# Pairs of experts as fp32 column strips between the units of a dense expert

## The reference

```python
def hierarchical_moe(h, w_rg, b_rg, w_re, b_re, w1, w3, w2):
    t = h.reshape(b * s, d)
    p_group = jax.nn.softmax((t @ w_rg + b_rg).astype(jnp.float32), axis=-1)
    g_val, g_idx = lax.top_k(p_group, 1)
    fine = (t @ w_re + b_re).astype(jnp.float32).reshape(-1, N_EXPERT_GROUPS, EXPERTS_PER_GROUP)
    ...
    for e in range(N_EXPERTS):
        y_e = (jax.nn.silu(t @ w1[e]) * (t @ w3[e])) @ w2[e]
        out = out + combine[:, e:e + 1] * y_e
    return out.reshape(b, s, d)
```

## Time and profile before

| | us |
| --- | --- |
| timed runs | 1611.56, 1608.8, 1608.3 |
| median | 1608.8 |
| span of the profiled execution | 1604.0 |
| PE busy in the span | 1547.5 (96%) |
| DVE, ACT busy | 1090.1 (68%), 838.2 (52%) |
| last matmul of the program, end | 1600.4 |

### The profile page before, as it was taken

How to read it: one execution, slowest core, us unless ns; L and a number is a source line. 1 busy time by engine, 2 the same in 40 slices (tenths; PEclk the granted TensorE clock), 3 DMA queues, 4 the chain that set the end, 5 groups by cost and what they waited for, 6 DMA issues and landing times.

```text
span 1604.0 us, 24065 instructions
## 1 busy us (share of the span) xinstructions
PE 1547.5 (96%) x8757; PEld 1261.9 (79%) x8757; DVE 1090.1 (68%) x1726; ACT 838.2 (52%) x1342; POOL 14.0 (1%) x36
## 2 busy tenths in 40 slices
PE   6999999999999999999999999998998999999999
PEld 3865558988888889888659999886776888889888
DVE  3447764854444446878977676887775687786894
ACT  4326554722322325688864544654453566666672
POOL 2000000000000000000010000000000000000000
PEclk9999999999999999999999999999999999999999
DMA  9588633422332332434525665543220789788792
GB/s 350 162 346 312 247 122 103 153 71 92 103 93 93 103 99 59 122 90 131 173 64 171 192 187 186 171 152 96 93 92 1 263 298 380 247 329 311 256 380 81
DMA packets 195799, 279.69 MB, mean 174 GB/s; under 512 B 12434, under 2 KB 111220, under 8 KB 190588
## 3 DMA queue, kind: packets, MB, share of 16 engines
q1 hardware_dynamic: 194308, 274.21, 50.6%
q0 software_dynamic: 1152, 4.19, 0.7%
q10 hardware_dynamic: 248, 0.09, 0.0%
HBM read 277.40 MB, written 1.05 MB: 174 GB/s over the span
## 4 chain that ended last, share of the span: by engine, by line
PE 76%; DVE 10%; ACT 7%; DMA 3%; issue 2%; SPq 0%; POOL 0%; DVEq 0%; ACTq 0%; POOLq 0%
PE bank L443 66%; DVE weights_lo L408 2%; PE bank L1540 2%; DMA ada_rows_in<-in_ada_w_dram 2%; PE bank L745 1%; ACT weights_hi L396 1%; PE bank L1381 1%; PE bank L1365 1%; DVE work L2781 1%; DVE softmax_cols L2648 1%; PE bank L1349 1%; ACT work L2118 1%; DVE x_and_ctx L590 1%; DMA stage<-in_lru_w_i_dram 1%; DVE work L2639 1%
## 5 line engine op out<-in xcount | busy, mean ns | idle before, releaser
L408 DVE TENSOR_TENSOR weights_lo<-stage,weights_hi 128x1024 fp32r<-128x1024 f32 x324 | 385.1, 1220 | 48.4 <-ACT weights_hi L396 44.6
L396 ACT ACTIVATE weights_hi<-stage 128x1024 fp32r<-128x1024 f32 x324 | 330.1, 1056 | 114.3 <-PE bank L443 69.4
L443 PE MATMUL bank<-act_hi,weights_hi 128*128 128x256 f32 (+1 forms) x1040 | 324.6, 312 | 1.3 <-DVE act_lo L553 1.0
L443 PE MATMUL bank<-act_lo,weights_hi 128*128 128x256 f32 (+1 forms) x1040 | 323.1, 311 | 0.0
L443 PE MATMUL bank<-act_hi,weights_lo 128*128 128x256 f32 (+1 forms) x1040 | 323.1, 311 | 0.0
L443 PE MATMUL bank<-weights_hi,ff_hi 128*128 128x512 f32 x568 | 221.6, 390 | 0.2 <-DVE ff_lo L3031 0.2
L443 PE MATMUL bank<-weights_hi,ff_lo 128*128 128x512 f32 x568 | 221.1, 389 | 0.0
L443 PE MATMUL bank<-weights_lo,ff_hi 128*128 128x512 f32 x568 | 221.0, 389 | 0.0
L443 PEld LDWEIGHTS bank<-act_hi,weights_hi 128*128 128x128 f32 x1040 | 198.3, 191 | 14.5 <-DVE act_lo L553 1.5
L443 PEld LDWEIGHTS bank<-act_lo,weights_hi 128*128 128x128 f32 x1040 | 198.3, 191 | 11.2
L443 PEld LDWEIGHTS bank<-act_hi,weights_lo 128*128 128x128 f32 x1040 | 198.3, 191 | 10.5
(11 more groups left out here) (404 smaller groups left out, 2018.5 us busy)
## 6 DMA issues: line engine op xcount, KB each, us to landing
stage<-in_mlp_w_dram SPq DMA_DIRECT2D x128, 512.0 KB, 4.0
stage<-in_w_dram SPq DMA_DIRECT2D x96, 512.0 KB, 6.1
ada_rows_in<-in_ada_w_dram SPq DMA_DIRECT2D x40, 1024.0 KB, 6.5
x_and_ctx<-in_w_dram SPq DMA_DIRECT2D x48, 512.0 KB, 5.9
work<-in_w_dram SPq DMA_DIRECT2D x48, 512.0 KB, 6.2
stage<-in_w_in_dram SPq DMA_DIRECT2D x32, 512.0 KB, 4.2
stage<-in_lru_w_in_dram SPq DMA_DIRECT2D x20, 512.0 KB, 3.9
stage<-in_attn_w_qkv_dram SPq DMA_DIRECT2D x12, 512.0 KB, 7.9
```

The lines of the kernel that those rows point to most:

```text
L396: act.eng.activation(whi[u % NRING][:], landing(act, u)[:], ACT.Copy).then_inc(sem("hi_ready"), 1)
L408: dve.eng.tensor_tensor(wlo[u % NRING][:], landing(dve, u)[:], whi[u % NRING][:].bitcast(F32), ALU.subtract).then_inc(sem("lo_ready"), 1)
L443: m = pe.eng.matmul(ps, l, r, start=start and j == 0, stop=stop and j == 2, skip_group_check=True)
```

## The change

The groups are ranked by their number of tokens. The largest (rank 0) is dense, ranks 1 and 2 have 128 slots each, and the smallest (rank 3, at most 64 tokens) has 64 slots. Its four experts, 12 to 15, are no steps of their own any more: they are taken as two **pairs** inside the steps of the dense experts 0 and 1. `STEPS` has 12 entries, p = 0 to 11: "both" at p = 0 and 5, slots experts 4 to 7 at p = 1 to 4 and 8 to 11 at p = 6 to 9, dense at p = 10 and 11.

In a "both" step a **pair call** follows each of the 12 units of the dense expert (`pair_up` after the 8 up units, `pair_down` after the 4 down units). It takes two units, one of each expert, straight from the landing buffers, neither split nor copied, and issues four fp32 matmuls of 512 columns. The 64 slots of the first expert stand in array columns 0 to 63, those of the second in 64 to 127; both write their half of one PSUM bank, 4 or 5 for up, 1 or 3 for down. Such a unit waits only for its landing, and its landing buffer is free again when PE has used it (`USED`), not when DVE has split it. ACT and DVE leave these units out (`WHOLE`, `SPLIT`, `split_index`).

The pair's hidden rows go through `tbuf`, `expert_turn` and a new ACT copy to `HP`. Its down product is copied to `YP` by ACT for the first pair; for the second DVE adds it (`pair_add`, two instructions), ACT makes the high half, DVE the low one (`pair_lo`), and the block is scattered in step 9. Blocks 0 and 1 are scattered in steps 8 and 11. The last dense expert's down product goes to banks 0 to 3, and DVE adds the last two dense experts at the end.

The up units are read with two neighbouring weight rows per partition (`twin`), so one descriptor covers 4 KB where it covered 2 KB. The order of the columns of `xn` is permuted to fit, and so are the router's weights (loaded in four transfers instead of two) and the norm's gain (a transfer of its own). In the gather loop 320 columns are made instead of 384, the third slots block has no low half, and splits stand after d = 1, 3 and 5 only. These are of units 0, 3 and 6, since units 1, 2, 4 and 5 belong to the first pair; the four splits behind the loop before are gone. `cw` is copied in three instructions instead of one.

The core of the diff:

```diff
+            if kind == "twin":
+                w, q = args
+                return (2, 512), w.rearrange("(q p e) n -> p q e n", p=P, e=2)[:, q]
...
+        STEPS = [("both", 0, 12), ("slots", 4), ("slots", 5), ("slots", 6), ("slots", 7), ("both", 1, 14), ("slots", 8),
+                 ("slots", 9), ("slots", 10), ("slots", 11), ("dense", 2), ("dense", 3)]
...
+        def step_units():
+            for p in range(LAST + 1):
+                yield p, 8
+                if p:
+                    yield p - 1, 4
+            yield LAST, 4
+        WHOLE = [w for p, n in step_units() for _ in range(n) for w in ([False, True, True] if paired(p) else [False])]
+        SPLIT = [u for u, whole in enumerate(WHOLE) if not whole]
...
-                if before >= 0:
-                    sp.eng.wait_ge(sem("lo_ready"), before + 1)
+                if before >= 0 and whole(before):
+                    sp.eng.wait_ge(sem(USED), before + 1)
+                elif before >= 0:
+                    sp.eng.wait_ge(sem("lo_ready"), split_index(before) + 1)
...
+        def pair_begin(pe, shape):
+            views = []
+            for _ in range(2):
+                u = pe.unit
+                pe.eng.wait_ge(*pe.at(*landed(pe, u)))
+                views.append(landing(pe, u)[:].rearrange("p (a b) -> p a b", a=shape[0]))
+                pe.unit += 1
+            return views
...
+            if tag == "n3":
+                src, xn = twin_cols(src), xn.rearrange("t (q e p) -> t q e p", q=4, e=2)
...
+                one = w[0].rearrange("(g e) k n -> e k g n", g=4)[e % 4]
+                return one[:, ds(group[e // 4], 1), :].rearrange("k g n -> k (g n)")
...
+                    for e in members(p):
+                        load_unit(sp, unit_of("twin", matrix(w, e), kq))
...
-                        mm = t.matmul(ps[:, 0:384], src[:, tt, d * P:d * P + P], SEL[:, tt, :],
+                        mm = t.matmul(ps[:, 0:320], src[:, tt, d * P:d * P + P], SEL[:, tt, 0:320],
...
+            def pair_up(p, j, kq):
+                key = ("hp", p, j)
+                if kq == 0:
+                    if plan.uses[4 + j]:
+                        t.wait_ge(*pe.bank_free(4 + j))
+                    pe.take(key, 4 + j)
+                w = pair_begin(pe, (2, 512))
+                for kk in range(2):
+                    k = 2 * kq + kk
+                    for e in range(2):
+                        mm = t.matmul(psum[4 + j][HD * e:HD * e + HD, :], GP[:, k, 0:HD], w[e][:, kk, :], start=k == 0,
+                                      stop=k == KT - 1, skip_group_check=True)
+                        if kk:
+                            mm.then_inc(sem(USED), 1)
+                pe.last = (USED, Affine(pe.unit, 0, 1))
+                plan.entry[key]["full"] = pe.last
...
+                        if paired(p):
+                            pair_up(p, j, kq)
...
+            def pair_down(p, f):
+                if f == 0:
+                    t.wait_ge(*pe.freed(("T", p)))
+                    for n in range(2):
+                        t.wait_ge(*pe.bank_free(1 + 2 * n))
+                        pe.take(("yp", p, n), 1 + 2 * n)
+                w = pair_begin(pe, (1, 1024))
+                for n in range(2):
+                    for m in range(2):
+                        mm = t.matmul(psum[1 + 2 * n][HD * m:HD * m + HD, :], HP[:, f, HD * m:HD * m + HD],
+                                      w[m][:, 0, n * 512:n * 512 + 512], start=f == 0, stop=f == 3,
+                                      skip_group_check=True)
+                        if n:
+                            mm.then_inc(sem(USED), 1)
+                pe.last = (USED, Affine(pe.unit, 0, 1))
+                for n in range(2):
+                    plan.entry[("yp", p, n)]["full"] = pe.last
...
+                turned = p and (not dense(p - 1) or paired(p - 1))
+                expert_up(p, 0, (lambda: expert_turn(p - 1)) if turned else None)
+                if p in SCATTER_STEP:
+                    scatter(SCATTER_STEP[p], 0)
+                    if dense(p):
+                        scatter(SCATTER_STEP[p], 1)
                 expert_up(p, 1)
-                if ends_block(p - 2):
-                    scatter(block_of(p - 2), 1)
+                if p in SCATTER_STEP and not dense(p):
+                    scatter(SCATTER_STEP[p], 1)
...
+            for p in range(LAST + 1):
+                if dense(p) and p:
+                    expert_hidden_hi(p - 1)
+                if paired(p):
+                    split_hi_to(act, before_up(p) + 5)
                 if ends_block(p - 2):
                     block_hi(block_of(p - 2))
+                if paired(p - 2):
+                    pair_y(p - 2)
                 expert_silu(p)
-                if p:
+                if p and not dense(p):
                     expert_hidden_hi(p - 1)
-                    split_hi(act, 4)
-                split_hi(act, 8)
+                split_hi_to(act, before_up(p + 1) + (3 if paired(p + 1) else 8))
...
+            v.scalar_tensor_tensor(out=group_keys[:, 0:4], in0=ps[:, 8:12], scalar=8.0, in1=prio[:], op0=ALU.mult,
                                    op1=ALU.add).then_inc(*dve.mark())
             v.wait_ge(*dve.own())
-            v.scalar_tensor_tensor(out=base, in0=upto, scalar=-128.0, in1=base, op0=ALU.mult, op1=ALU.add).then_inc(*dve.mark())
-            v.wait_ge(*dve.own())
-            v.tensor_tensor(slot, ps[:, 0:8].rearrange("p (t g) -> p t g", t=2),
-                            base.unsqueeze(1).to_broadcast([P, 2, 4]), ALU.add).then_inc(*dve.free("count"))
+            v.max(out=ranked, in_=group_keys[:]).then_inc(*dve.mark())
+            v.wait_ge(*dve.own())
+            v.max_index(out=order[:], in_max=ranked, in_values=group_keys[:]).then_inc(*dve.mark("group_order"))
...
-                v.scalar_tensor_tensor(out=G3L[:, d, :], in0=ps[:, TX:384], scalar=colA[:, d, 0:1],
-                                       in1=G3H[:, d, :].bitcast(F32), op0=ALU.mult,
                                        op1=ALU.subtract).then_inc(*dve.free(("gather", d)))
-                if d % 2:
+                if d in (1, 3, 5):
                     split_lo(dve, 1)
-            split_lo(dve, 4)
...
-            v.tensor_copy(cw, ps[:, 0:12]).then_inc(*dve.free("slot_weight"))
+            v.tensor_copy(cw, ps[:, 0:8]).then_inc(*dve.mark())
+            for e in range(2):
+                part = slice(HD * e, HD * e + HD)
+                i = v.tensor_copy(cwp[part, :], ps[part, 8:12].rearrange("p (a b) -> p b a", b=2)[:, e, :])
+                i.then_inc(*(dve.free("slot_weight") if e else dve.mark()))
...
+                if p - 2 == EXPERT_PAIRS[1]:
+                    pair_add(p - 2)
                 if dense(p - 2):
                     expert_sum(p - 2, 0)
                     expert_sum(p - 2, 1)
                 if p:
                     expert_hidden_lo(p - 1)
-                    split_lo(dve, 2)
-                if ends_block(p - 2):
-                    block_sum(block_of(p - 2), 0)
-                split_lo(dve, 6 if p else 4)
+                    split_lo_to(dve, before_up(p + 1) - 2)
+                if p - 2 == EXPERT_PAIRS[1]:
+                    pair_lo()
+                if p in SCATTER_STEP:
+                    block_sum(SCATTER_STEP[p], 0)
+                    if dense(p):
+                        block_sum(SCATTER_STEP[p], 1)
+                split_lo_to(dve, before_up(p + 1) + (3 if paired(p + 1) else 4))
                 expert_product(p)
-                if ends_block(p - 2):
-                    block_sum(block_of(p - 2), 1)
-                split_lo(dve, 4)
-            if dense(LAST - 1):
-                expert_sum(LAST - 1, 0)
-                expert_sum(LAST - 1, 1)
+                if p in SCATTER_STEP and not dense(p):
+                    block_sum(SCATTER_STEP[p], 1)
+                split_lo_to(dve, before_up(p + 1) + (3 if paired(p + 1) else 8))
```

More of the change, by code:

```diff
@@ L3214, in _ @@
[L3214 to L3220 removed]
+            ranked, slot, one = rt(9, 8), rt(11, 2, 4), rt(13, 4)
+            wide, ahead = rt(10, 4), rt(14, 4, 4)
```

280 lines of the change are left out of this document (165 added, 115 removed).

## The result

| | median us (runs) | ratio to before, 95% interval |
| --- | --- | --- |
| before | 1609.4 (1608.3 to 1611.6) | |
| after | 1617.8 (1613.7 to 1618.5) | 1.0049 [1.0035, 1.0062] |

The change makes the kernel 0.5% slower, where 0.6% faster was forecast (1617.8 us against 1599.4). The profiled execution of after spans 1612.0 us, 8.0 more than that of before; the sum had 1594.6.

The account below looks back on a forecast made before the run. PE, busy throughout the expert stage, was taken as the bound. 1604.0 - 15.8 - 0.9 (two turns) + 4.9 + 2.0 + 0.4 = 1594.6 span, plus 4.8 from span to median, gives 1599.4 us; range 1589 to 1610.

Parts of the forecast that it names:

- the sum: Whole kernel: all terms added to the span before, 1604.0, giving a span of 1594.6 us.
- part 1: Pairs on PE: 24 calls of 2.06 us with overlapping strips replace four slots experts, a gain of 15.8 us.
- rival of strips in turn: Pair calls: strips run one after another, 3.75 us a call, 1640 us in all; chance 0.05.
- part 2: DVE and ACT behind the pairs: waits of PE in steps 1, 2, 6 and 7, together +4.9 us.
- PE wants it at 5.44 + 0.44 + 5.44 = 11.3: Step 2: first down split, ready at 12.0 after the last pair call, is wanted at 11.3; PE waits 0.7 us.
- PE idle over 10 us in the stage: Expert stage: sign that the forecast was wrong; it expected PE idle of 4 to 6 us.
- The landing: Last two up units behind a pair: the nearly empty queue takes 3.7 us from issue to landing.
- rival of larger handover waits: Behind the pairs: units land after 6.0 to 6.3 us at four places, so 1609 us; chance 0.15.
- part 3: Front, gather loop to first dense unit: late third split +1.0 and clock +1.0, together +2.0 us.
- gap of 3.5 before `slot_weight`: Front: PE waits some 3.5 us before slot_weight and may lose its clock.
- The clock term: Front: half speed for 3 us costs 1.5, of which two thirds is taken, +1.0 us.
- Small terms: Norm row with permuted writes +0.4 us; router and gain transfers, 4 KB rows, gather and tail 0.

Follow-up runs that it names:

- e4_both: Kernel after the change with one gather-loop split, early dense sums, and step 7's pair_add, high half and pair_lo behind the splits PE awaits; 1600.5 us, ratio 0.9937.
- e2_sums: Kernel after the change, with the sums of dense experts 0 and 1 ahead of the next step's last three up splits; 1609.0 us, ratio 1.0000.
- e5_notwin: Kernel after the change, with up units read in 2 KB rows and norm, gain and router order as before; 1617.4 us, ratio 1.0053.
- e6_serial: Kernel after the change, with the four matmuls of each up call issued strip by strip instead of in turns; span 1614.3 us.
- e8_both_last_first: e4_both with the last pair calls also ahead of the last dense unit; 1598.9 us, ratio 0.9940.
- e9_warm: Kernel after the change, with idle matmuls on PE before d = 4 (8) and d = 6 (3) of the gather loop; 1616.5 us, ratio 1.0043.
- e10_one_strip: Kernel after the change, with both experts of the up calls in one strip for all but the first weight row; span 1635.6 us.
- e12_best_warm: e8_both_last_first with idle matmuls in the gather loop (8 and 3) as well; 1598.8 us, ratio 0.9939.
- e1_front: Kernel after the change, with one split in the gather loop instead of three; 1614.7 us, ratio 1.0025.
- e7_last_first: Kernel after the change, with the last pair call of both steps before the last dense unit, loads included; 1616.2 us, ratio 1.0043.
- e11_warm_all: e9_warm with 12 more idle matmuls before slot_weight; 1614.0 us, ratio 1.0032.

## Why the prediction was wrong

- **The calls (part 1): right.** 2.05 and 2.14 against 2.06; strips overlap, loads are hidden, the change of shape costs what rows 4 and 6 gave. The rival of strips in turn was priced at a call of 3.75; forced into one strip, it is 3.65 in its row and 3.58 from start to start.
- **The waits behind the pairs (part 2): wrong, and this is the step that turned the sign.** The failed step is "PE wants it at 5.44 + 0.44 + 5.44 = 11.3". I took the first down unit as the only one who waits for DVE's row of last splits, sums, hidden low. But the transposes take bank 5, which the sums free, and PE wants them at 5.44. The sums' second instruction ended 10.7 after the last call (the sum's own numbers give 3.7 + 1.1 + 2.5 + 1.4, 8.7). So even with my own landing time the wait in step 2 is over 3 us, not 0.7. The sign that the prediction set for this part, PE idle over 10 us in the stage, came: 14.1. In before the splits ahead of the sums were never late (the last ended 1304.99, with PE at the transposes at 1308.00), so that dependence was satisfied and couldn't be seen as a wait in any row; it stood in the code alone.
- **The landing: undersized.** I took 3.7 for an empty queue. The queue wasn't empty (DMA share 0.94 from 1332 to 1334, 0.85 in the next 2 us): the unit lands 5.6 and 6.2 after issue. That is the rival of larger handover waits, whose mechanism was right in this and whose place was wrong in the same way as mine. Together the two made 12.4, and 3.3 of clock, where the sum had 3.6 for steps 2 and 7; steps 1 and 6 had some 1.1 and 2.0 instead of 0.2 and 1.1, and the 0.9 at the start of step 10 wasn't in the sum.
- **The front (part 3): right in kind, wrong in the unit.** I looked at the third split; the second one, of the unit that lands fourth, was in the way already. The stage starts 3.3 later instead of 1.0 (of which 1.3 is the clock at the router and 1.2 in `slot_weight`), and 2.4 of half clock in the first dense unit instead of 1.0. The gap of 3.5 before `slot_weight` wasn't there as such (0.98 in its row): PE waited 2.3 and 1.1 earlier in the gather loop and 1.0 there. The clock term was the right worry, far too small: 1.0 against the 8 us of this execution.
- **Small terms.** The norm row is 0.75 as before: 0 instead of 0.4. The rest stayed at nothing.

With the sums in time, one split in the gather loop and the pair's block off the path, the change gives 0.6%, what the forecast had. That the number is the same is in part chance, since PE still idles 6.9 in that stage against the 4.9 of the sum. But the gain of the pairs was there, and was given back in waits for an order on DVE that the change had left as it was, and in the clock behind them.

What stays open: the split of the 18 us that e4_both gains over after between its three edits (8 and 4 alone; the rest would be `pair_add` and what the clock adds, which is argued and not shown), and which part of the 5.6 to a landing is the start of a transfer and which its neighbours in the queue.

## What to carry to other kernels

When a change makes a producer late, don't look for the first consumer of its data only: list everything queued behind it on its engine, and for each the semaphore or bank it frees and who takes that, also where the trace of before shows no wait. A slack that was never used up has no row. And price an idle gap of PE at more than its length: here the clock was halved behind the gaps of 5.0 and 6.7 us, which cost 1.7 each on top, and not behind the 3.0 of e2_sums.

## What was not expected of the hardware

- Two 64-column fp32 strips overlap in both orders tried in a call of eight passes: 1.94 in turns, 1.94 one strip after the other, 3.65 in one strip.
- The same code at the router, with the same 1.67 us of waiting before it, ran its 24 matmuls at full clock in some executions (3.0 us; before, e4_both, e5_notwin, e6_serial, e8_both_last_first, e9_warm, e10_one_strip, e12_best_warm) and at half in others (4.6; after, e1_front, e2_sums, e7_last_first, e11_warm_all). This 1.5 us, 0.1%, can be a part of the scatter of up to 0.6% in the times of one kernel, and one profile can't show it. It also means that the 1.3 at the router in the account of the 8.0 needn't be due to the change. From after, at half clock, a matmul of 256 columns every 0.21:

```profile
1236.06 0.41 PE L513 MATMUL bank<-act_hi,w_small_lo 128*80 128x256 f32 x1
1236.28 0.41 PE L513 MATMUL bank<-act_hi,w_small_hi 128*80 128x256 f32 x1
```
